# An encoder layer on eight cores: value products behind every attention visit, a plan made with other durations, and one more weight slot

## The chip, the cores and the metric

The program runs on all eight cores of one Trainium2 chip. Every core does the same work on its own two of sixteen sequences; the cores exchange nothing. The metric is the device time in microseconds (us) of the slowest core, as the median of the timed runs. An engine is named as in the profile: PE is the matmul engine (TensorE), ACT ScalarE, DVE VectorE, POOL GpSimd, SP the engine that issues the transfers.

## What is computed

The reference is one layer of an encoder, cut here to its steps. A sequence has 2048 tokens of width 1024.

```
n1 = rmsnorm(h)                         # h: (2048, 1024) a sequence
q, k, v, u, gates = split(n1 @ w_in)    # 8 query heads, 2 key/value heads of 64; u and gates
q, k = rope(rmsnorm(q)), rope(rmsnorm(k))
a = softmax(q k^T / 8) v @ w_attn_up    # every query sees all 2048 keys
p = (multiscale_pool(u) @ pool_w * pool_scale) @ w_pool_up
h = h + (sigmoid(g_a) * a + sigmoid(g_p) * p) @ w_out
h = h + cross_attention(rmsnorm(h), rmsnorm(mem))     # 256 memory tokens, 4 heads of 256
h = h + square(relu(rmsnorm(h) @ w_ff1)) @ w_ff2      # 4096 wide
out = rmsnorm(h)
```

## The kernel before

**Tiles and stages.** Everything is kept with the model's width on the 128 partitions and tokens along the free dimension. A core works on eight blocks of 512 tokens (two sequences, four each). After a prologue (keys, values and pooled input of the first sequence, the folding of the memory into weights) each block goes through stages that the code names A (gates, up and output projections), B (cross attention) and F (the feed-forward layer, FF1 and then FF2). Weights come as fp32 from `wst` the first time or times, are cast to bf16 into a slot of the pool W, stored to `wsc`, and read back from there later. How many blocks read a weight as fp32 before the bf16 copy serves is in the table `LATE`.

**Attention visits.** Attention of a block is cut into 32 visits of 256 keys for two query heads, eight visits to each of four chunks; there are 256 visits in all. A visit (`visit`, in `attention_steps`) has four score matmuls of 64 rows, two at a time side by side (the rows of the trace with `ps<-S_p,KV_p`, x4), into all four PSUM banks of the pool E. One exponential on ACT (line 1242) reads those four banks and writes a tile P in a slot of M2. The value products (`ps<-M_p,KV_p`) multiply P with the values, four matmuls of 64 columns for each visit, two at a time. `GROUP` says after how many visits they are issued: with 2, the products of two visits stand together behind the scores of each second visit, "glued" to them, so that nothing comes between. The next visit's scores write the same four banks and so wait for the exponential of the one before.

**Sums of a softmax.** They are built on DVE, two additions for each visit (lines 1253 and 1254), or on PE as products with ones (`ps<-M_p,ones_bf`). `TAIL_PE` says for which blocks the last visits of each chunk are summed on PE: for block (0, 0) the last two.

**Modes of the array.** Scores use halves of the rows, value products halves of the columns, other matmuls the whole array. `split_columns` looks at PE's finished order: a whole-array operation that comes after value products is issued as two matmuls of 64 columns side by side (line 764), until the next score matmuls; the others are issued whole (line 768).

**What sets the order.** The whole program is recorded as operations, each with a place in a nominal order (`items`): the blocks' stages follow each other, and attention of the next block is laid over them by tables of places (`SHARE`, `SHARE1`, `QUERY`, `TILES`). `schedule` then plays all five engines forward, with a duration for each kind of operation (`act_t`, `dve_t`, `pool_t`, the costs in `copy_any`, `DMA_LAT` for a transfer) and with a random jitter from `SEED`, and gives each engine a fixed order. An operation with several possible engines (casts, additions) goes to the one that the plan finds free. The pools W, M2, M1 and S1 have a fixed number of slots in SBUF, and the plan gives each value its slot. `keep_warm` looks at the finished plan and puts matmuls of ones (`ps<-ones_bf`) into PE's longer planned gaps. The chip runs the five orders with semaphores between them.

Of the kernel before, what the change touches and what calls it, by code (L numbers as in the profile page):

```python
# [49 lines left out]


def GROUP(s, tb):
    return 2


def AUX(query, attention, tile, blocks):

    aux = [(attention(*blocks[0]), ("o1", 0.0), ("o1", 1.0)),
           (query(*blocks[1]), ("o2", 0.0), ("o2", 0.2))]
    steps, k = attention(*blocks[1]), 0  # L60
    for n, lo, hi in SHARE1:
        part, k = steps[k:k + n], k + n
        aux.append((part, lo, hi))
    for b in range(2, 8):
        aux.append((query(*blocks[b]), (f"A{b - 1}", QUERY[0]), (f"A{b - 1}", QUERY[1])))
        steps, k = attention(*blocks[b]), 0
        for n, lo, hi in SHARE:
            part, k = steps[k:k + n], k + n
            aux.append((part, (lo[0] + str(b - 1), lo[1]), (hi[0] + str(b - 1), hi[1])))
    for t, (a, b) in enumerate(TILES):  # L70
        aux.append((tile(t), a, b))
    return aux
# [8 lines left out]
DMA_BW = 380.0  # L81
DMA_FIX = 250.0
BACKLOG = 5000.0
DMA_LAT = 2000.0
DMA_ISSUE = 420.0
ALT_BIAS = 300.0
LEAD0 = 4
SHARE = ((6, ('A', 0.7), ('B', 0.06)), (6, ('B', 0.06), ('F', 0)), (6, ('F', 0), ('F', 0.53)), (16, ('F', 0.53), ('F', 0.958)))
SHARE1 = ((34, ('o2', 0.49), ('F0', 0.988)),)
QUERY = (0.05, 0.42)  # L90
TILES = ((('F1', 0.0), ('F1', 0.31)), (('A2', 0.2), ('F2', 0.0)), (('F2', 0.2), ('F2', 0.41)), (('A3', 0.26), ('A3', 0.94)))
NORM1 = (1, 4)
# [577 lines left out]
def build_core(info=None):  # L670
# [13 lines left out]
    G = Graph()  # L684
    st = ExitStack()
    with st:
        def sb(name, shape, dt):
            return st.enter_context(nc.sbuf_tensor(name, shape, dt))

        SIZES = dict(W=(10, 2048, BF16), M2=(14, 1024, F32), M1=(28, 512, F32), S1=(44, 512, BF16), KV=(4, 2048, BF16))  # L690
        tens = {k: sb(k + "_p", [128, n, w], dt) for k, (n, w, dt) in SIZES.items()}
        ps = st.enter_context(nc.psum_tensor("ps", [128, 8, 512], F32))
        pools = {k: v[0] for k, v in SIZES.items()}
# [89 lines left out]
        def copy_any(dst, src, n, R, W, psum=True, scale=None, engs=("act", "dve", "pool"), rate=1.0):  # L783
            def fn_of(eng):
                def fn(e):
                    if eng == "act":
                        if scale is None:
                            return e.activation(out=dst(), in_=src(), func=AF.Copy)  # L788
                        return e.activation(out=dst(), in_=src(), func=AF.Copy, scale=scale())
                    if scale is None:  # L790
                        return e.tensor_copy(out=dst(), in_=src())  # L791
                    return e.tensor_scalar(out=dst(), in0=src(), scalar1=scale(), scalar2=None, op0=ALU.mult)
                return fn
            fns = {e: fn_of(e) for e in engs}
# [1134 lines left out]
```

How the kernel before makes its waits and increments, by code:

```python
    def do_waits(eng, ws):  # L624
        for w in ws:
            if w[0] == "d":
                eng.wait_ge(dsem[w[1]], w[2])
            else:
                k = ms[w[1]]
                eng.wait_ge(esem[w[1].eng][k // SEM_CAP], k % SEM_CAP + 1)
# [1 line left out]
    def run(e, eng):  # L632
        for o in order[e]:
            if o.mms is not None:
                for m, ws in zip(o.mms, plan[o]):
                    do_waits(eng, ws)
                    ins = m["fn"](eng, "halves" in m)
            else:
                do_waits(eng, plan[o])
                ins = o.fn(eng)
            if o.dma is not None:
                ins.then_inc(dsem[o.key[0]], 16)
            elif o in ms:
                ins.then_inc(esem[e][ms[o] // SEM_CAP], 1)
# [17 lines left out]
    @block.sync  # L662
    def _(eng):
        run("sp", eng)
        for s, c in dcount.items():
            eng.wait_ge(dsem[s], c * 16)
```

## Time and profile before

| | us |
|---|---|
| median of three runs | 2161.4 (2159.53 to 2165.31) |
| the profiled execution | 2164.5 |
| span of its slowest core (core 1) | 2162.9 |
| spans of the eight cores | 2151.9 to 2162.9 |
| PE busy | 2099.0 (97%) |
| DVE, ACT, POOL busy | 1665.7, 1376.6, 402.8 |

The rows of the trace are of core 1. A view "by window" gives the busy time of each engine in a stretch; the time line gives start, length, engine, line, tiles and count of merged instructions, and in brackets the idle time before them with what ended it. Matmuls are pipelined, so a PE row is drawn longer than the time to the next start: durations on PE are read from start to start.

### The profile page before, as it was taken

Reading aid. Unit: us, or ns where it says so; the run is one execution under the profiler, and the core shown is the slowest. Engines: PE = TensorE matmul, PEld = TensorE weight load, DVE = VectorE, ACT = ScalarE, POOL = GpSimd, SP = SyncE. Lnnn points to the kernel's source line nnn. Section 1 sums busy time; section 2 is a strip of 40 time slices with the busy share of each in tenths; the row PEclk is TensorE's granted clock in tenths of the full one; section 3 lists DMA queues with packets and bytes.
Section 4 is the critical chain, followed back from the end, with each engine's and each line's share of the span. In section 5 each row is a group of like instructions: output and inputs, shape, how many; then the busy total and the mean of one; then the engine's idle time right before and its main releaser. Section 6 shows DMA issues by size and latency. Waiting matters only on the chain.

```text
span 2162.9 us, 49417 instructions; the slowest of 8 cores (2151.9 to 2162.9 us)
## 1 busy us (share of the span) xinstructions
PE 2099.0 (97%) x18391; PEld 1210.8 (56%) x18391; DVE 1665.7 (77%) x2358; ACT 1376.6 (64%) x1710; POOL 402.8 (19%) x305
## 2 busy tenths in 40 slices
PE   9898999999999999999999999999999999999998
PEld 5543544445456654566644764467445754476678
DVE  5976788778887798877888778778877788876663
ACT  6787677657965679546775468546764478545431
POOL 1321344222430131003410121002110021000200
PEclk9999999999999999999999999999999999999999
DMA  8977997999777865458634683457534763367446
GB/s 262 315 256 246 312 300 232 304 320 310 249 262 253 280 228 177 165 195 276 231 108 137 224 269 113 137 192 243 182 126 154 256 214 114 134 219 261 135 160 201
DMA packets 152442, 473.29 MB, mean 219 GB/s; under 512 B 17040, under 2 KB 21264, under 8 KB 152208
## 3 DMA queue, kind: packets, MB, share of 16 engines
q1 hardware_dynamic: 152208, 470.14, 66.3%
q8 instruction: 151, 2.47, 0.4%
q14 instruction: 83, 0.68, 0.1%
HBM read 399.82 MB, written 70.25 MB: 217 GB/s over the span
## 4 chain that ended last, share of the span: by engine, by line
PE 82%; DMA 6%; ACT 4%; DVE 4%; issue 3%; SPq 1%; POOL 1%; DVEq 0%; ACTq 0%; POOLq 0%
PE ps L764 44%; PE ps L768 37%; DMA M_p<-wst 4%; ACT M_p L1242 2%; DMA wsc<-W_p 1%; SPq L776 1%; ACT W_p L788 1%; DMA M_p<-pdd 0%; POOL M_p L864 0%; DMA M_p<-xT 0%; ACT M_p L876 0%; DVE M_p L1253 0%; DVE M_p L1254 0%; DVE M_p L881 0%; DVE S_p L1447 0%
## 5 line engine op out<-in xcount | busy, mean ns | idle before, releaser
L1242 ACT ACTIVATE M_p<-ps 128x2048 bf16<-128x2048 f32 x256 | 480.2, 1876 | 265.5 <-PE ps L768 259.2
L764 PE MATMUL ps<-S_p,W_p 128*64 128x512 bf16 (+1 forms) x6136 | 620.3, 357 | 4.0 <-POOL W_p L791 1.4
L764 PEld LDWEIGHTS ps<-S_p,W_p 128*64 128x64 bf16 x6136 | 369.2, 110 | 232.8 <-issue 11.8
L764 PE MATMUL ps<-M_p,W_p 128*64 128x512 bf16 (+1 forms) x4976 | 455.1, 337 | 8.4 <-ACT W_p L788 3.8
L768 PE MATMUL ps<-S_p,W_p 128*128 128x512 bf16 (+1 forms) x2372 | 445.9, 344 | 4.6 <-DVE W_p L791 2.2
L764 PEld LDWEIGHTS ps<-M_p,W_p 128*64 128x64 bf16 x4976 | 310.9, 110 | 133.2 <-issue 14.3
L1253 DVE TENSOR_TENSOR M_p<-M_p 128x1024 f32<-128x1024 f32 x216 | 271.2, 1256 | 114.0 <-ACT M_p L1242 110.0
L864 POOL TENSOR_TENSOR M_p<-M_p 128x512 f32<-128x512 f32 x115 | 164.6, 1433 | 1036.6 <-ACT M_p L855 1001.8
L768 PEld LDWEIGHTS ps<-S_p,W_p 128*128 128x128 bf16 x2372 | 224.7, 98 | 221.6 <-issue 46.9
L1254 DVE TENSOR_TENSOR M_p<-M_p 128x1024 f32<-128x1024 f32 x216 | 281.6, 1304 | 11.4 <-DVE M_p L1253 0.5
L1500 ACT ACTIVATE M_p<-M_p 128x512 bf16<-128x512 f32 x256 | 157.0, 627 | 160.4 <-DVE M_p L1498 158.4
L1498 DVE SCALAR_TENSOR_TENSOR M_p<-ps,M_p 128x512 f32<-128x512 f32 x256 | 174.0, 688 | 66.9 <-PE ps L764 37.2
L791 POOL CAST W_p<-M_p 128x1024 bf16<-128x1024 f32 x96 | 119.6, 1253 | 330.8 <-DMA M_p<-wst 141.8
L768 PE MATMUL ps<-S_p,KV_p 64*128 64x512 bf16 x1024 | 155.1, 381 | 24.9 <-ACT M_p L1242 21.8
L768 PE MATMUL ps<-M_p,W_p 128*128 128x256 bf16 (+1 forms) x1168 | 178.1, 308 | 0.5 <-DVE M_p L1433 0.3
L855 ACT ACTIVATE M_p<-M_p 128x512 f32<-128x512 f32 x216 | 129.5, 624 | 57.5 <-DVE M_p L1402 25.9
L768 PEld LDWEIGHTS ps<-M_p,W_p 128*128 128x128 bf16 x1168 | 111.0, 98 | 65.7 <-issue 16.7
L768 PE MATMUL ps<-M_p,KV_p 128*64 128x512 bf16 x1024 | 136.1, 386 | 0.0
L1322 ACT ACTIVATE M_p<-ps,nbg 128x512 f32<-128x512 f32 x128 | 86.8, 686 | 57.5 <-PE ps L764 54.7
L788 ACT ACTIVATE W_p<-M_p 128x1024 bf16<-128x1024 f32 x72 | 75.4, 1054 | 72.4 <-DMA M_p<-wst 32.1
L1597 DVE TENSOR_TENSOR M_p<-ps,M_p 128x512 f32<-128x512 f32 x112 | 77.1, 688 | 54.1 <-PE ps L764 40.9
L768 PEld LDWEIGHTS ps<-S_p,KV_p 64*128 64x128 bf16 x1024 | 30.2, 94 | 114.2 <-issue 114.2
(105 smaller groups left out, 1985.3 us busy)
## 6 DMA issues: line engine op xcount, KB each, us to landing
W_p<-wsc SPq DMA_DIRECT2D x490, 512.0 KB, 4.7
M_p<-wst SPq DMA_DIRECT2D x182, 512.0 KB, 10.0
wsc<-W_p SPq DMA_DIRECT2D x77, 512.0 KB, 9.4
M_p<-xT SPq DMA_DIRECT2D x120, 256.0 KB, 9.4
outT<-M_p SPq DMA_DIRECT2D x56, 256.0 KB, 5.9
n1d<-M_p SPq DMA_DIRECT2D x28, 256.0 KB, 5.6
M_p<-n1d SPq DMA_DIRECT2D x28, 256.0 KB, 7.2
pdd<-M_p SPq DMA_DIRECT2D x14, 256.0 KB, 3.1
```

Of the source, the lines that this page charges most:

```text
L764: ins = e.matmul(out()[64 * k:64 * k + 64], lhsT=lhsT()[:, 64 * k:64 * k + 64], rhs=rhs(), start=start, stop=stop, skip_group_check=True, ...
L768: return e.matmul(out(), lhsT=lhsT(), rhs=rhs(), start=start, stop=stop, skip_group_check=True, **kw)
L788: return e.activation(out=dst(), in_=src(), func=AF.Copy)
L791: return e.tensor_copy(out=dst(), in_=src())
L855: A(lambda e: e.activation(out=ap(sq), in_=src(), func=AF.Square), 512, False, R, [sq])
L864: TT(lambda e: e.tensor_tensor(out=ap(out), in0=ap(acc), in1=ap(sq), op=ALU.add), [acc, sq], [out])
L1242: A(lambda e: e.activation(out=b16(P).rearrange("p (a n) -> p a n", n=512), in_=ps[:, 0:4, :], func=AF.Exp, scale=0.125), 2048, True, S, [P])
L1253: D(lambda e: e.tensor_tensor(out=ap(acc), in0=ap(acc), in1=lo(), op=ALU.add), 1024, [P, acc], [acc], port=True)
L1254: D(lambda e: e.tensor_tensor(out=ap(acc), in0=ap(acc), in1=hi(), op=ALU.add), 1024, [P, acc], [acc], port=True)
L1322: A(lambda e, b=b, i=i: e.activation(out=ap(Et)[:, i * 512:(i + 1) * 512], in_=ap(b), func=AF.Exp, bias=nbg[:, i * 8 + j:i * 8 + j + 1], s ...
L1498: D(lambda e: e.scalar_tensor_tensor(out=ap(rl), in0=ap(b), scalar=0.0, in1=ap(r), op0=ALU.max, op1=ALU.mult), 512, [b, r], [rl])
L1500: A(lambda e: e.activation(out=hq(H, 2 * hf, 2), in_=ap(rl), func=AF.Square), 512, False, [rl], keys)
```

## The change

`GROUP` becomes 1: the four value products of each visit are issued right behind the scores of the next one. `TAIL_PE` is widened to block (0, 1), whose last four visits of each chunk are summed on PE instead of DVE. The plan gets other durations: `DMA_LAT` 4000 ns instead of 2000, `pool_t` 440 ns instead of 300 for its fixed part, a cast on POOL 380 instead of 200. W has 11 slots instead of 10, S1 40 instead of 44 (the same bytes). The tables of places, `LATE` and `SEED` have other numbers.

```diff
 def GROUP(s, tb):
-    return 2
+    return 1
...
-        for n, lo, hi in SHARE:
+        for n, lo, hi in {2: SHARE2, 3: SHARE3}.get(b, SHARE):
...
-DMA_LAT = 2000.0
+DMA_LAT = 4000.0
...
-SHARE = ((6, ('A', 0.7), ('B', 0.06)), (6, ('B', 0.06), ('F', 0)), (6, ('F', 0), ('F', 0.53)), (16, ('F', 0.53), ('F', 0.958)))
-SHARE1 = ((34, ('o2', 0.49), ('F0', 0.988)),)
-QUERY = (0.05, 0.42)
...
+SLOTS = (11, 14, 28, 40)
+SHARE = ((3, ('A', 0.7), ('B', 0.12)), (9, ('B', 0.12), ('F', 0.12)), (6, ('F', 0.12), ('F', 0.59)), (10, ('F', 0.59), ('F', 0.864)), (6, ('F', 0.864), ('F', 0.958)))
...
+SHARE1 = ((34, ('o2', 0.67), ('F0', 0.965)),)
+QUERY = (0.09, 0.56)
...
-SEED = 7958
+SEED = 194
...
-TAIL_PE = {(0, 0): 2}
+TAIL0 = 2
+TAIL1 = 4
+TAIL_PE = {(0, 0): TAIL0, (0, 1): TAIL1}
...
-LATE.update({("G", i): i % 2 for i in range(8)})
-LATE.update({("FA", i): i % 3 for i in range(16)})
+LATEG = (1, 0, 0, 0, 0, 1, 1, 1)
+LATE.update({("G", i): LATEG[i] for i in range(8)})
+LATEF = (0, 1, 2, 0, 1, 1, 0, 1, 2, 0, 1, 2, 0, 1, 2, 0)
+LATE.update({("FA", i): LATEF[i] for i in range(16)})
...
-        SIZES = dict(W=(10, 2048, BF16), M2=(14, 1024, F32), M1=(28, 512, F32), S1=(44, 512, BF16), KV=(4, 2048, BF16))
+        SIZES = dict(W=(SLOTS[0], 2048, BF16), M2=(SLOTS[1], 1024, F32), M1=(SLOTS[2], 512, F32), S1=(SLOTS[3], 512, BF16), KV=(4, 2048, BF16))
...
         def pool_t(n):
-            return 300.0 + n * 1.9
+            return 440.0 + n * 1.9
...
-            cost = dict(act=act_t(n, psum, scale is not None), dve=dve_t(n, rate), pool=200.0 + n * 0.85)
+            cost = dict(act=act_t(n, psum, scale is not None), dve=dve_t(n, rate), pool=380.0 + n * 0.85)
```

The rows below are of the programs as built, equal instructions merged. Lines of the changed kernel are seven higher (775 for 768, 771 for 764). In the first place, PE in the middle of a block's feed-forward layer, rows with `S_p,KV_p` are the scores of one visit, `M_p,KV_p` value products. Before:

```order
L768 MATMUL ps<-S_p,KV_p 128x512 x4
L768 MATMUL ps<-S_p,W_p 128x512 x16
L768 MATMUL ps<-S_p,KV_p 128x512 x4
L768 MATMUL ps<-M_p,KV_p 64x512 x8
L764 MATMUL ps<-S_p,ones_bf 64x512 x2
L768 MATMUL ps<-S_p,KV_p 128x512 x4
L768 MATMUL ps<-S_p,W_p 128x512 x72
```

PE at the same stage, as changed:

```order
L775 MATMUL ps<-S_p,KV_p 128x512 x4
L775 MATMUL ps<-M_p,KV_p 64x512 x4
L775 MATMUL ps<-M_p,ones_bf 64x512 x2
L771 MATMUL ps<-S_p,W_p 64x512 x16
L775 MATMUL ps<-S_p,KV_p 128x512 x4
L775 MATMUL ps<-M_p,KV_p 64x512 x4
L771 MATMUL ps<-ones_bf 64x512 x6
L771 MATMUL ps<-S_p,W_p 64x512 x32
```

Two visits that stood with only eight value products and a sum between them are no longer there; every score row is followed by four value products, and the weight matmuls between visits are now in the split form.

The second place is PE at the start of attention in the prologue, the first visits of block (0, 0). Before:

```order
L768 MATMUL ps<-S_p,KV_p 128x512 x4
L768 MATMUL ps<-ones_bf 128x512 x8
L768 MATMUL ps<-S_p,KV_p 128x512 x4
L768 MATMUL ps<-M_p,KV_p 64x512 x8
L764 MATMUL ps<-ones_bf 64x512 x8
L768 MATMUL ps<-S_p,KV_p 128x512 x4
L768 MATMUL ps<-ones_bf 128x512 x9
L768 MATMUL ps<-S_p,KV_p 128x512 x4
L768 MATMUL ps<-M_p,KV_p 64x512 x8
L764 MATMUL ps<-S_p,W_p 64x512 x80
```

PE at the same visits, as changed:

```order
L775 MATMUL ps<-S_p,KV_p 128x512 x4
L775 MATMUL ps<-M_p,KV_p 64x512 x4
L771 MATMUL ps<-ones_bf 64x512 x12
L775 MATMUL ps<-S_p,KV_p 128x512 x4
L775 MATMUL ps<-M_p,KV_p 64x512 x4
L771 MATMUL ps<-ones_bf 64x512 x12
L775 MATMUL ps<-S_p,KV_p 128x512 x4
L775 MATMUL ps<-M_p,KV_p 64x512 x4
L771 MATMUL ps<-ones_bf 64x512 x4
L771 MATMUL ps<-S_p,W_p 64x512 x48
```

The value products now stand in every gap, and one visit fewer has no weight matmuls behind it. Ones are still in the gaps.

The third place is DVE in the feed-forward layer of the first block, where weights are still cast. `L1505` reads an FF1 result out of PSUM (`L1498` before), `L1258` and `L1270` belong to the softmax sums and outputs. As changed:

```order
L799 TENSOR_SCALAR S_p<-M_p,vec_sb 128x512
L798 CAST W_p<-M_p 128x1024 x2
L871 TENSOR_TENSOR S_p<-M_p 128x512
L798 CAST W_p<-M_p 128x1024 x4
L1505 SCALAR_TENSOR_TENSOR M_p<-ps,M_p 128x512 x2
L798 CAST W_p<-M_p 128x1024
L1505 SCALAR_TENSOR_TENSOR M_p<-ps,M_p 128x512
L798 CAST W_p<-M_p 128x1024
L1258 TENSOR_TENSOR M_p<-M_p 128x1024
```

DVE at that stage before:

```order
L1254 TENSOR_TENSOR M_p<-M_p 128x1024
L1498 SCALAR_TENSOR_TENSOR M_p<-ps,M_p 128x512 x3
L1253 TENSOR_TENSOR M_p<-M_p 128x1024
L1254 TENSOR_TENSOR M_p<-M_p 128x1024
```

Weight casts have come to DVE (41 without a scale in the program instead of 10, with 69 instead of 96 on POOL and 66 instead of 72 on ACT; two fewer in all), and additions for the softmax sums have left it (400 instead of 432 of lines 1253 and 1254).

## Rows read from the trace of the kernel before

**Rows 1.** The page: span, busy time and share of each engine
```profile
span 2162.9 us, 49417 instructions; the slowest of 8 cores (2151.9 to 2162.9 us)
PE 2099.0 (97%) x18391; PEld 1210.8 (56%) x18391; DVE 1665.7 (77%) x2358; ACT 1376.6 (64%) x1710; POOL 402.8 (19%) x305
```
**Rows 2.** By window: start:end, length, busy us of each engine, clock, DMA share
```profile
0.00:500.00 500.00, 463.75 (x3255) 228.78 (x3257) 381.64 (x500) 361.09 (x455) 142.07 (x114) 0.99 0.90 284
500.00:1200.00 700.00, 686.73 (x6151) 393.48 (x6149) 569.60 (x814) 470.06 (x601) 150.24 (x110) 1.00 0.66 219
1200.00:2163.00 963.00, 948.48 (x8995) 588.56 (x8989) 714.50 (x1046) 545.42 (x655) 110.45 (x81) 1.00 0.55 185
```
**Rows 3.** The page's chain that ended last, by engine
```profile
PE 82%; DMA 6%; ACT 4%; DVE 4%; issue 3%; SPq 1%; POOL 1%; DVEq 0%; ACTq 0%; POOLq 0%
```
**Rows 4.** Waits of PE: waiting <- waited for, us in total, times, longest
```profile
PE ps L768 <- ACT M_p L1242: 21.8, 21, 2.4
PE ps L768 <- DVE W_p L791: 3.8, 5, 1.5
PE ps L764 <- ACT W_p L788: 3.8, 2, 3.0
PE ps L764 <- DMA M_p<-pdd: 2.0, 1, 2.0
PE ps L764 <- DMA W_p<-wsc: 1.6, 2, 1.1
```
**Rows 5.** Time line of PE in a feed-forward layer: start us, length, instructions
```profile
1363.94 0.61 PE L768 MATMUL ps<-S_p,KV_p 64*128 64x512 bf16 x4
1364.48 1.05 PE L768 MATMUL ps<-M_p,KV_p 128*64 128x512 bf16 x8
...
1366.67 0.61 PE L768 MATMUL ps<-S_p,KV_p 64*128 64x512 bf16 x4 [0.93 <-ACT M_p L1242]
1367.27 15.70 PE L768 MATMUL ps<-S_p,W_p 128*128 128x512 bf16 x72
1382.90 0.61 PE L768 MATMUL ps<-S_p,KV_p 64*128 64x512 bf16 x4
1383.44 1.05 PE L768 MATMUL ps<-M_p,KV_p 128*64 128x512 bf16 x8
1384.33 13.98 PE L764 MATMUL ps<-S_p,W_p 128*64 128x512 bf16 x128
1398.24 0.60 PE L768 MATMUL ps<-S_p,KV_p 64*128 64x512 bf16 x4
```
**Rows 6.** Time line of PE in FF2, matmuls of 256 columns
```profile
1434.29 3.66 PE L764 MATMUL ps<-M_p,W_p 128*64 128x256 bf16 x64
1437.88 0.61 PE L768 MATMUL ps<-S_p,KV_p 64*128 64x512 bf16 x4
1438.42 3.67 PE L768 MATMUL ps<-M_p,W_p 128*128 128x256 bf16 x32
1442.02 0.61 PE L768 MATMUL ps<-S_p,KV_p 64*128 64x512 bf16 x4
```
**Rows 7.** Time line of PE at the first visits
```profile
102.23 0.61 PE L768 MATMUL ps<-S_p,KV_p 64*128 64x512 bf16 x4 [1.47 <-ACT M_p L1242]
102.77 2.12 PE L768 MATMUL ps<-ones_bf 128*128 128x512 bf16 x9
107.24 0.61 PE L768 MATMUL ps<-S_p,KV_p 64*128 64x512 bf16 x4 [2.35 <-ACT M_p L1242]
```
**Rows 8.** By source line, duration ns min/median/max; by group: busy us, mean ns
```profile
L1242 ACT ACTIVATE M_p<-ps x256: 1854/1878/1904, 93.5 to 1956.6; 128x2048 bf16<-128x2048 f32 x128
L791 DVE CAST W_p<-M_p x10: 685/694/1017, 18.1 to 439.5; 128x1024 bf16<-128x1024 f32 x10
L1253 DVE TENSOR_TENSOR M_p<-M_p 128x1024 f32<-128x1024 f32 x216 | 271.2, 1256 | 114.0 <-ACT M_p L1242 110.0
L791 POOL CAST W_p<-M_p 128x1024 bf16<-128x1024 f32 x96 | 119.6, 1253 | 330.8 <-DMA M_p<-wst 141.8
```

More of the change, by code:

```diff
@@ L87 @@
 LEAD0 = 4
-SHARE = ((6, ('A', 0.7), ('B', 0.06)), (6, ('B', 0.06), ('F', 0)), (6, ('F', 0), ('F', 0.53)), (16, ('F', 0.53), ('F', 0.958)))
-SHARE1 = ((34, ('o2', 0.49), ('F0', 0.988)),)
-QUERY = (0.05, 0.42)
-TILES = ((('F1', 0.0), ('F1', 0.31)), (('A2', 0.2), ('F2', 0.0)), (('F2', 0.2), ('F2', 0.41)), (('A3', 0.26), ('A3', 0.94)))
+SLOTS = (11, 14, 28, 40)
+SHARE = ((3, ('A', 0.7), ('B', 0.12)), (9, ('B', 0.12), ('F', 0.12)), (6, ('F', 0.12), ('F', 0.59)), (10, ('F', 0.59), ('F', 0.864)), (6, ('F', 0.864), ('F', 0.958)))
+SHARE2 = ((3, ('A', 0.7), ('B', 0.096)), (9, ('B', 0.096), ('F', 0.12)), (6, ('F', 0.12), ('F', 0.47)), (8, ('F', 0.47), ('F', 0.804)), (8, ('F', 0.804), ('F', 0.958)))
+SHARE3 = ((6, ('A', 0.7), ('B', 0.12)), (8, ('B', 0.12), ('F', 0.24)), (4, ('F', 0.24), ('F', 0.47)), (9, ('F', 0.47), ('F', 0.744)), (7, ('F', 0.744), ('F', 0.958)))
+SHARE1 = ((34, ('o2', 0.67), ('F0', 0.965)),)
+QUERY = (0.09, 0.56)
+TILES = ((('F1', 0.1), ('F1', 0.41)), (('A2', 0.2), ('F2', 0.3)), (('F2', 0.1), ('F2', 0.17)), (('A3', 0.22), ('A3', 0.74)))
 NORM1 = (1, 4)
```

## The prediction

> **What bounds the kernel now.** I began with the page: PE is busy for 97% of the span, no other engine for more than 77% [rows 1], and the chain that ended last runs through PE for 82% [rows 3]. So the time is PE's own work plus the places where it stands still. The windows say where: in the first 500 us PE is idle for 500 − 463.75 = 36.3 us, with the DMA engines 90% busy; in the next 700 us for 13.3; in the last 963 for 14.5, the tail after the last matmul among it [rows 2]. To that idle time belong the matmuls of ones that only fill planned gaps. Counted in the program's order there are 220 of them at 0.216 us, 47.5 us. Then the waits of PE: by far the largest is that of a score matmul for the exponential of the visit before, 21.8 us in 21 waits; weights that are cast or loaded too late cost 3.8, 3.8 and 1.6, a load of pooled input 2.0 [rows 4]. The change must be read as: what does it add to PE's work, and which of the stalls does it end?
>
> **PE's work.** Three things change, all counted in the two orders.
>
> Sums of block (0, 1): 4 chunks × 4 visits × 4 matmuls = 64 more, 32 pairs. A pair takes as long as one whole matmul, 0.216 us (below). 32 × 0.216 = **+6.9 us**. On DVE the same visits lose 32 additions of 1.256 us [rows 8], 40 us; DVE isn't the bound, so that counts only where PE waits for it.
>
> Changes of mode: from rows to columns or to the whole array and back. Before, 520; with the change 512. Although value products now stand behind each visit, the count doesn't double: before, a visit without value products had two changes (whole to rows, rows to whole), one with them also two, since what follows value products is issued in split form. Each costs about 0.1 us: four scores take 0.54 us to the next start instead of 2 × 0.216 [rows 5]. 8 × 0.1 = **−0.8 us**.
>
> The split form: 9,491 pairs in the changed program, 5,980 before, so 3,511 matmuls are issued as two. Its price is in the rows. With 512 columns, 72 whole ones go from 1367.27 to 1382.90, 15.63 us, and 64 pairs from 1384.33 to 1398.24, 13.91 us [rows 5]. Less 0.1 for the change of mode that follows each, this is 0.2157 and 0.2158 us. With 256 columns, 64 split ones take 3.59 us and 32 whole ones 3.60 [rows 6]. So **0**, with at most 1 ns either way, 3.5 us, for the range. It has to be 0 in both forms, as nearly the whole program now runs split.
>
> The Trainium skill speaks against this one (TensorEngine Tiling, section Tile-to-Partition Mapping: column tiling disables the fast loading of weights; and TensorE: Matmul & The Clock Gate, section Packing small matmuls: a weight load overlaps running matmuls only where its row group differs, which for column halves it does not). By its figure of 64/1.2 = 53 ns for a load of 64 columns, an exposed load in each of 3,511 more pairs would add 186 us. The rows disagree: the pairs of [rows 5, 6] show no such time, and half the program already ran that way.
>
> **Waits for the exponential.** The scores of a visit use the four banks that the exponential before them reads. From scores to the next scores takes at least 1366.67 − 1363.94 = 2.73 us [rows 5]: 0.54 of scores, 1.88 of exponential [rows 8], the rest semaphores. I take 2.75. Where PE has less real work than that between two score rows, it must stand still or run ones, whatever the rest of the plan does. So I walked both orders with 0.216 us for a matmul or pair of 512 columns, 0.109 for 256 and 0.1 for a change of mode, leaving out the ones. Before, 23 of the 255 gaps between visits fall short, by 20.1 us together. The row that the profile has for it, 21.8 us in 21 waits [rows 4], is that size. Twelve of these 23, 13.2 us, are before 500 us, some with ones in them, as at 102.23 (1.47 us left) and 107.24 (2.35) [rows 7]; the other eleven, 6.9 us, are later and recur from block to block, as at 1366.67 with 0.93 us [rows 5]. With the change 9 gaps fall short, by 8.7 us, all before 200 us. The gain is in two parts: value products of 0.43 us are now in every gap instead of 0.86 in every other one, and the other tables spread the visits. 20.1 − 8.7 = **−11.4 us**. The bounds are 0 (the time is lost to the next wait) and −15, as a wait like that of 2.35 us [rows 7] is longer than the shortfall of its gap.
>
> **Ones.** 195 of them instead of 220, −5.4 us at most. 3.7 of it lie in the same short gaps and are counted above; **−1.7 us** for the rest. They are not work, they stand where the plan sees nothing to do, so this is a hint that the plan has fewer holes and not more than that.
>
> **Transfers, casts and slots.** With 4000 ns for the latency the plan asks for loads earlier, and with an eleventh slot it can. What there is to win is what PE waits for: 2.0 + 1.6 for loads and 3.8 + 3.8 for casts, 11.2 us [rows 4]. A slot of W held by a value is what a load waits for, and a tenth more of them moves a load about a tenth earlier; most waits are for casts in the first 500 us, where the DMA engines are 90% busy [rows 2] and no slot gives them more. The POOL casts are planned at 1.25 us instead of 1.07 and take 1.253 on average [rows 8], so the plan is right about them now on average and moves 27 away. I take **−3 us**, between −11 and +4. The 31 more casts on DVE are 31 × 0.694 = 21.5 us [rows 8] against the 40 that left; **−1 us** for DVE, between −4 and +10. S1 is smaller but free: followed through the changed order, never fewer than 2 of its 40 slots are empty. The bytes read stay the same but for two loads of fp32 weights.
>
> **The sum.** 6.9 − 0.8 + 0 − 11.4 − 1.7 − 3 − 1 = −11.0 us. The profiled execution would take 2164.5 − 11.0 = 2153.5. It is 3.1 above the median, and the difference is taken off that: 2161.4 − 11.0 = **2150.4 us**, 0.5% faster. The cores of one execution span 2151.9 to 2162.9 [rows 1] with the same program, so each term of a few us is at the size of what one core differs from another. What a measurement can tell from no change is about 0.3%, 6.5 us.
>
> **The rivals.** *The gain is given back in the first 500 us.* There the DMA engines are 90% busy and PE idles for 36 us [rows 2] because weights aren't there; the exponential's waits of that stretch (13.2 of the 20.1 us before, 8.7 after) then only turn into waits for weights. What is left is the rest of the spacing, 6.9 us, against 6.9 − 0.8 of new work: −0.8, **2160.6 us**. For it speaks the DMA share, against it that only 11 us of PE's waits name a load or a cast.
>
> *The traced durations mend the early stage too.* If the orders now fit what really happens, part of the 36.3 us of idle time before 500 us and of the ones there goes. With 40% of it, 14.5 us, on top of the sum, it comes to **2136 us**. Against it speaks again the DMA share.
>
> *DVE becomes what PE waits for, in the first feed-forward layer.* Its order there has runs of up to six casts with an addition between them, ahead of the instructions that read FF1's results out of PSUM: 6 × 0.694 + 1.26 = 5.4 us, while PE fills one of four banks in 8 × 0.216 = 1.73 us, so it can run 6.9 us ahead. It decides from the point where a run is late by more than 1.5 us, as DVE is 381.6/500 = 76% busy there [rows 2] and a cast of the fp32 tiles can't start before its load has landed; behind it all results queue. Four or five such stalls of 4 us, 18 us, would make it −11.0 + 18 = +7, **2168.5 us**, slower.
>
> *The split form costs something after all.* At 5 ns for a pair, 3,511 × 5 = 17.6 us, it is slower by more than noise: 2150.4 + 17.6 = **2168 us**; from 3.1 ns on the gain is gone. The rows leave room for 1 ns. An exposed load in each pair, as the skill's rule above has it, would show at once in [rows 5, 6] and has under 1% of this.
>
> *The plan doesn't do what its tables say*: a recorded order is fixed, so value products are where the order shows them; this has no chance of its own.
>
> **How the numbers follow.** My forecast, 2143 to 2157 us around 2150.4, 0.45. Given back in the early stage, 2156 to 2165: 0.26. The early stage mended too, 2130 to 2143: 0.15. DVE: 0.11. The split form: 0.03. From the forecast's case a little falls within 0.3% (above 2154.9), from the second a little below it. Faster by over 0.3%: 0.57. Within: 0.30. Slower: 0.13. The range of 8 in 10 takes in the first three but for the far end of the mended case, and the DVE case at its lower price: 2136 to 2167.
>
> **What would show it.** In the profile after: PE's waits for line 1249 (the exponential) at 9 to 12 us instead of 21.8, and none of about 1 us in the later blocks; 64 pairs of 512 columns still at 13.8 us and the FF2 pieces at 3.6; idle time of PE before 500 us near 33; waits of PE for casts below 8; the later blocks 1 to 2 us shorter each. It would be wrong if PE's waits for DVE lines (1505 above all) grow by over 5 us between 200 and 500 us, if the idle time before 500 us falls by more than 10, or if the waits for the exponential stay at 20 with the gaps filled, which would mean that ACT's own queue, not the spacing, sets them.

## The result, and the profile of the changed kernel

| | before | changed |
|---|---|---|
| median us | 2160.84 (4 runs, 2159.53 to 2165.31) | 2139.34 (4 runs, 2137.71 to 2140.53) |
| ratio | 1 | 0.989, 95% interval 0.9862 to 0.9919 |
| profiled execution | 2164.5 | 2137.7 |
| spans of the eight cores | 2151.9 to 2162.9 | 2126.3 to 2136.1 |

The change makes the kernel 21.5 us faster, 1.0%. The prediction was 2150.4, 11.0 us faster. The profiled executions lie a little above the one median and below the other, so they differ by 26.8. The ratios here and below leave out executions in which the cores of one die show a lower granted clock.

First the page of the changed kernel, against [rows 1, 3, 8]: span, busy time and share of each engine, the chain by engine, and two groups (busy us, mean ns, idle time before them).

```profile
span 2136.1 us, 56390 instructions; the slowest of 8 cores (2126.3 to 2136.1 us)
PE 2096.2 (98%) x21918; PEld 1262.8 (59%) x21918; DVE 1628.9 (76%) x2330; ACT 1386.7 (65%) x1729; POOL 388.0 (18%) x280
...
PE 87%; DVE 5%; DMA 4%; issue 2%; ACT 1%; SPq 1%; DVEq 0%; POOL 0%; ACTq 0%; POOLq 0%
...
L1260 DVE TENSOR_TENSOR M_p<-M_p 128x1024 f32<-128x1024 f32 x200 | 251.1, 1256 | 124.7 <-ACT M_p L1249 121.8
...
L798 POOL CAST W_p<-M_p 128x1024 bf16<-128x1024 f32 x69 | 86.9, 1266 | 279.0 <-DMA M_p<-wst 134.9
```

PE has 19% more instructions but about the same busy time; its share of the chain rose from 82 to 87%. Then the windows of [rows 2] again (length, busy time of PE, PEld, DVE, ACT and POOL, granted clock, DMA share, GB/s).

```profile
0.00:500.00 500.00, 476.48 (x4080) 250.23 (x4082) 358.15 (x503) 368.90 (x470) 117.47 (x93) 1.00 0.93 291
500.00:1200.00 700.00, 694.69 (x7626) 420.60 (x7624) 567.97 (x807) 473.08 (x604) 143.91 (x105) 1.00 0.70 222
1200.00:2140.00 940.00, 925.00 (x10220) 591.97 (x10216) 702.75 (x1022) 544.77 (x657) 126.62 (x83) 1.00 0.57 183
```

PE's idle time before 500 us fell from 36.3 to 23.5 us, though the DMA engines are busier there (0.93 instead of 0.90). From 500 to 1200 us it fell from 13.3 to 5.3. PE's waits (us in total, times, longest), against [rows 4]:

```profile
PE ps L775 <- ACT M_p L1249: 8.1, 11, 1.7
PE ps L771 <- DVE W_p L798: 4.6, 3, 3.1
PE ps L771 <- DMA W_p<-wsc: 3.2, 1, 3.2
PE ps L775 <- ACT S_p L910: 1.7, 2, 1.3
PE ps L771 <- DVE M_p L1604: 1.5, 2, 1.2
...
PE ps L775 <- DVE M_p L1505: 1.4, 3, 0.9
```

The wait for the exponential went from 21.8 to 8.1 us (8.4 with one that another matmul takes). By stage it went from 15.6 to 8.4 before 500 us and from 6.3 to nothing after it. The waits that name a weight's cast or a load are still 7.8 in these rows. All of them, small ones too, are 14.3 before and 9.1 now; all other waits fell from 18.3 to 13.3. A later block, PE's time line, against [rows 5]:

```profile
1364.41 0.60 PE L775 MATMUL ps<-S_p,KV_p 64*128 64x512 bf16 x4
1364.94 0.62 PE L775 MATMUL ps<-M_p,KV_p 128*64 128x512 bf16 x4
1365.40 5.35 PE L771 MATMUL ps<-S_p,W_p 128*64 128x512 bf16 x48
1370.68 0.60 PE L775 MATMUL ps<-S_p,KV_p 64*128 64x512 bf16 x4
1371.21 0.62 PE L775 MATMUL ps<-M_p,KV_p 128*64 128x512 bf16 x4
1371.67 10.53 PE L771 MATMUL ps<-S_p,W_p 128*64 128x512 bf16 x96
1382.13 0.60 PE L775 MATMUL ps<-S_p,KV_p 64*128 64x512 bf16 x4
```

No gap is left in it: 48 pairs, 10.46 us less 0.1 for the change of mode, are 0.216 us each, and the wait of 0.93 us is gone.

**Where the time went.** I took every PE row of the slowest core from its start to the next start, and put into the last line what exceeds the undisturbed duration of its kind (idle time, and rows that run at half the clock):

| us of the slowest core | before | changed |
|---|---|---|
| work of PE, with changes of mode | 2022.5 | 2028.7 (+6.2) |
| ones | 47.5 | 42.1 (−5.4) |
| standing, before 500 us | 49.5 | 33.3 |
| standing, 500 to 1200 us | 20.7 | 11.2 |
| standing, after 1200 us | 12.8 | 11.3 |
| standing, all | 83.1 | 55.8 (−27.3) |

The rest, start and tail, is the same in both. The sum is −26.5, for spans that differ by 26.8. These are the slowest cores of one execution each, but the standing time of every core before is longer than that of any core now.

A part of the standing time is no wait at all. Before, after the wait of 2.35 us at 107.24 [rows 7], PE worked on at half its clock. The windows of before at that place, in the columns of above:

```profile
100.00:108.00 8.00, 4.19 (x27) 1.41 (x25) 7.83 (x10) 5.61 (x5) 1.56 (x2) 1.00 1.00 306
108.00:112.00 4.00, 4.00 (x24) 1.81 (x22) 1.15 (x1) 2.88 (x3) 0.00 (x0) 0.57 0.99 262
112.00:116.00 4.00, 4.00 (x42) 2.08 (x38) 3.56 (x4) 2.32 (x3) 0.00 (x0) 1.00 0.99 278
```

The four busy microseconds from 108 hold 24 matmuls, the next four 42. The granted clock is 0.57 on average, so the lower of the two levels (1.2 of 2.4 GHz) for most of it. Core 1 had four such stretches of 3.4 us before (from 108.1, 193.5, 476.8 and 739.6), each at or just behind a stop of PE of 2.0 to 3.0 us; at half speed they cost at most 4 × 1.7 = 6.8 us. The changed kernel's slowest core has one. On its time line:

```profile
462.41 0.60 PE L775 MATMUL ps<-M_p,ones_bf 128*64 128x512 bf16 x4
466.19 3.45 PE L771 MATMUL ps<-M_p,W_p 128*64 128x512 bf16 x16 [3.18 <-DMA W_p<-wsc]
469.57 0.60 PE L775 MATMUL ps<-S_p,KV_p 64*128 64x512 bf16 x4
```

Eight pairs take 3.38 us instead of 1.73: the wait of 3.18 for a load costs 4.8. But not every stop is followed by such a stretch. The same core's stop of 3.15 us at 212 isn't. Its end on the time line, and the window behind it with clock 1.00:

```profile
214.73 0.62 PE L771 MATMUL ps<-W_p,S_p 128*64 128x512 bf16 x4 [3.15 <-DVE W_p L798]
214.70:219.00 4.30, 3.92 (x32) 1.72 (x34) 3.06 (x5) 2.18 (x2) 1.75 (x2) 1.00 0.68 220
```

Over the eight cores of both executions, 37 stops of PE last 2 us or more (between 50 and 2120 us); 23 of them have a stretch at the lower clock at or within 3.5 us of their end and 14 have none. The slowest cores are extremes: the median of the eight cores has 3.4 us of such losses before and 1.7 now.

### The profile page after: what moved, and what is told of

Its sections match the earlier page's. It is cut to its first block, busy times and chain, and to the rows that moved or that the text cites. A ratio compares the mean times of both kernels' runs of the same rounds, so it can differ in the third digit from the quotient of the medians.

```text
span 2136.1 us, 56390 instructions; the slowest of 8 cores (2126.3 to 2136.1 us)
## 1 busy us (share of the span) xinstructions
PE 2096.2 (98%) x21918; PEld 1262.8 (59%) x21918; DVE 1628.9 (76%) x2330; ACT 1386.7 (65%) x1729; POOL 388.0 (18%) x280
## 4 chain that ended last, share of the span: by engine, by line
PE 87%; DVE 5%; DMA 4%; issue 2%; ACT 1%; SPq 1%; DVEq 0%; POOL 0%; ACTq 0%; POOLq 0%
PE ps L771 71%; PE ps L775 16%; DMA M_p<-wst 2%; DVE M_p L1261 1%; DMA wsc<-W_p 1%; DVE M_p L1260 1%; DMA W_p<-wsc 1%; DMA M_p<-memT 1%; SPq L783 0%; ACT M_p L1249 0%; DVE M_p L1685 0%; DVE W_p L798 0%; DVE M_p L1258 0%; DVE S_p L888 0%; DVE M_p L888 0%
## 5 line engine op out<-in xcount | busy, mean ns | idle before, releaser
L771 PE MATMUL ps<-S_p,W_p 128*64 128x512 bf16 (+1 forms) x10608 | 1035.7, 350 | 6.8 <-DVE W_p L798 1.5
L771 PEld LDWEIGHTS ps<-S_p,W_p 128*64 128x64 bf16 x10608 | 629.2, 110 | 378.5 <-issue 22.1
L1249 ACT ACTIVATE M_p<-ps 128x2048 bf16<-128x2048 f32 x256 | 479.7, 1874 | 259.7 <-PE ps L775 244.0
L771 PE MATMUL ps<-M_p,W_p 128*64 128x512 bf16 (+1 forms) x7168 | 617.0, 326 | 5.0 <-DMA W_p<-wsc 3.2
L771 PEld LDWEIGHTS ps<-M_p,W_p 128*64 128x64 bf16 x7168 | 425.6, 110 | 174.4 <-issue 14.0
L1260 DVE TENSOR_TENSOR M_p<-M_p 128x1024 f32<-128x1024 f32 x200 | 251.1, 1256 | 124.7 <-ACT M_p L1249 121.8
L1261 DVE TENSOR_TENSOR M_p<-M_p 128x1024 f32<-128x1024 f32 x200 | 264.2, 1321 | 9.6 <-DVE M_p L1260 0.5
L1505 DVE SCALAR_TENSOR_TENSOR M_p<-ps,M_p 128x512 f32<-128x512 f32 x256 | 173.0, 685 | 50.9 <-PE ps L771 45.9
L775 PE MATMUL ps<-M_p,KV_p 128*64 128x512 bf16 x1024 | 159.3, 391 | 0.3 <-ACT M_p L1249 0.3
L798 POOL CAST W_p<-M_p 128x1024 bf16<-128x1024 f32 x69 | 86.9, 1266 | 279.0 <-DMA M_p<-wst 134.9
L1604 DVE TENSOR_TENSOR M_p<-ps,M_p 128x512 f32<-128x512 f32 x112 | 76.9, 687 | 49.6 <-PE ps L771 47.8
L795 ACT ACTIVATE W_p<-M_p 128x1024 bf16<-128x1024 f32 x66 | 69.1, 1053 | 61.2 <-DMA M_p<-wst 26.9
L775 PEld LDWEIGHTS ps<-M_p,KV_p 128*64 128x64 bf16 x1024 | 36.4, 108 | 107.5 <-issue 107.1
L1332 ACT ACTIVATE M_p<-M_p 128x1024 f32<-128x1024 f32 x64 | 67.6, 1057 | 4.4
L1334 ACT ACTIVATE M_p<-M_p 128x1024 f32<-128x1024 f32 x64 | 67.4, 1054 | 3.4 <-ACT M_p L1332 0.4
L1409 DVE TENSOR_TENSOR M_p<-ps,M_p 128x512 f32<-128x512 f32 x64 | 44.0, 688 | 30.5 <-PE ps L771 16.5
```

What stands on the lines that cost most here:

```text
L771: ins = e.matmul(out()[64 * k:64 * k + 64], lhsT=lhsT()[:, 64 * k:64 * k + 64], rhs=rhs(), start=start, stop=stop, skip_group_check=True, ...
L775: return e.matmul(out(), lhsT=lhsT(), rhs=rhs(), start=start, stop=stop, skip_group_check=True, **kw)
L1249: A(lambda e: e.activation(out=b16(P).rearrange("p (a n) -> p a n", n=512), in_=ps[:, 0:4, :], func=AF.Exp, scale=0.125), 2048, True, S, [P])
L1260: D(lambda e: e.tensor_tensor(out=ap(acc), in0=ap(acc), in1=lo(), op=ALU.add), 1024, [P, acc], [acc], port=True)
L1261: D(lambda e: e.tensor_tensor(out=ap(acc), in0=ap(acc), in1=hi(), op=ALU.add), 1024, [P, acc], [acc], port=True)
L1505: D(lambda e: e.scalar_tensor_tensor(out=ap(rl), in0=ap(b), scalar=0.0, in1=ap(r), op0=ALU.max, op1=ALU.mult), 512, [b, r], [rl])
```

## The experiments

Three theories stand against each other. *Spacing*: the gain is the filled gaps between score rows. *Durations and slots*: the plan's new latency, POOL durations and the eleventh slot make things ready in time, more than the waits that name them show. *Luck*: any new order with another seed moves the time by as much.

The kernels ran on three other chips; each ratio is to the kernel before on the same chip (medians there 2157.1, 2168.5 and 2167.0). The changed kernel was not run again on these chips, so "against changed" is (ratio − 0.989) × 2161 us, and carries the uncertainty of both ratios, about ±7 us. "Short gaps" is the sum that the walk of the prediction gives for the order. "All waits" adds up the waits of PE on the slowest core of the profiled execution (in e2 7.6 of the 31.2 us name no releaser; PE rows are missing from that core's trace).

| kernel | ratio, 95% | against changed | short gaps | ones | all waits |
|---|---|---|---|---|---|
| before | 1 | +24 | 20.1 | 47.5 | 54.4 |
| changed | 0.989, 0.9862 to 0.9919 | 0 | 8.7 | 42.1 | 30.8 |
| e1 before, all split | 1.0008, 0.9992 to 1.0024 | | 19.8 | 47.5 | 46.7 |
| e2 changed, whole | 0.9987, 0.9974 to 1.0 | +21 | 8.0 | | 31.2 |
| e3 before, GROUP 1 | 1.0091, 1.0066 to 1.0115 | | 15.9 | 52.9 | 52.9 |
| e4 changed, seed 7958 | 0.9932, 0.9908 to 0.9957 | +9 | 6.8 | 40.2 | 34.5 |
| e5 before, seed 194 | 1.0021, 0.9998 to 1.0043 | | 17.9 | 47.7 | 52.0 |
| e6 before, new durations | 0.9988, 0.9975 to 1.0002 | | 16.0 | 47.3 | 54.4 |
| e7 changed, old durations | 1.0002, 0.9986 to 1.0018 | +24 | 13.8 | 44.5 | 52.1 |
| e8 changed, old tables | 1.0016, 0.9992 to 1.004 | +27 | 15.4 | 45.6 | 52.7 |
| e9 changed, old latency | 0.9977, 0.9963 to 0.9992 | +19 | 9.8 | 41.7 | 49.0 |
| e10 changed, old POOL durations | 0.9916, 0.99 to 0.9931 | +6 | 19.1 | 44.7 | 36.2 |
| e11 changed, ten slots | 0.9989, 0.9977 to 1.0002 | +21 | 12.4 | 45.6 | 44.1 |
| e12 changed, no TAIL1 | 0.9958, 0.9942 to 0.9973 | +15 | 15.5 | 54.9 | 36.8 |

### The split form

e1 changes the kernel before so that, from the first scores on, every whole-array operation is issued as halves, as far as the changed kernel goes with it.

```diff
-        if mode == "c" and whole_array(o):
+        if mode != "f" and whole_array(o):
+            mode = "c"
```

> The kernel before in the same order, but the whole-array matmuls behind score matmuls are issued as two column halves too (some 3,670 more split ones, 512 changes of mode instead of 520). Theory that a pair costs what a whole matmul costs: -0.8 us for the changes of mode, so 2155 to 2165 us, no difference. Rival, that a pair costs 2 to 5 ns more: 7 to 18 us slower. Rival, that split matmuls are where the change gained: 10 us faster or more.

Measured 1.0008, no difference. Its PE time line at the place of [rows 5]:

```profile
1358.08 0.61 PE L769 MATMUL ps<-S_p,KV_p 64*128 64x512 bf16 x4 [0.92 <-ACT M_p L1243]
1358.67 15.73 PE L765 MATMUL ps<-S_p,W_p 128*64 128x512 bf16 x144
1374.34 0.60 PE L769 MATMUL ps<-S_p,KV_p 64*128 64x512 bf16 x4
```

72 pairs take 15.67 us to the next start, the 72 whole matmuls of before 15.63. And the wait of 0.92 us stays, as nothing here fills that gap.

e2 takes the split form out of the changed kernel, and so puts a change of mode behind each visit's value products: 788 instead of 512.

```diff
-        if mode == "c" and whole_array(o):
-            for m in o.mms:
-                m["halves"] = True
-        else:
-            mode = o.mms[-1]["mode"]
+        mode = o.mms[-1]["mode"]
```

> The changed kernel in its own order, but everything that can be whole is issued whole, so that PE goes back from columns to the whole array behind each visit's value products: 788 changes of mode instead of 512. At 0.096 us each that is 26.5 us slower than the changed kernel, 2166 us or 0.2% above the kernel before. Rival, that the split form has a price of its own of 2 ns or more: at most 8 us slower than the changed kernel, 2147. The granted clock should not differ.

Measured 0.9987, some 21 us above the changed kernel. Its PE time line:

```profile
1302.63 0.61 PE L771 MATMUL ps<-S_p,KV_p 64*128 64x512 bf16 x4
1303.17 0.62 PE L771 MATMUL ps<-M_p,KV_p 128*64 128x512 bf16 x4
1303.72 1.90 PE L771 MATMUL ps<-M_p,W_p 128*128 128x512 bf16 x7
```

Value products last 0.55 us to the next start instead of 0.46. On the median core of the profiled executions PE's work grew by 25.8 us, 0.093 for each of the 276 changes, while the standing time fell by 11. This fits changes of mode that lie inside waits, which isn't shown place by place. So the split form is what makes GROUP 1 affordable, and no price of it shows.

### Value products behind each visit, alone

```diff
 def GROUP(s, tb):
-    return 2
+    return 1
```

> The kernel before with nothing changed but the value products behind each visit (GROUP 1); the plan is made anew with the old tables, durations and slots. Walked through its order, gaps between visits that are shorter than 2.75 us sum to 15.9 us instead of 19.8, the changes of mode to 0.8 less; ones go up from 220 to 245. Theory of the spacing: -4.7 us, 2156. Theory that issuing value products behind each visit is most of the gain by itself (shorter lives of P, more even work): -15 us or more, 2146 or below. Theory that the plan's other inputs carry the gain: within 5 us of before.

Measured 1.0091: **slower** by 19.7 us, though the walk has 4 us less of short gaps, and the waits for the exponential did fall (21.8 to 13.7 us). The plan made with the old tables got other holes: 245 ones instead of 220 (+5.4 us) and 8.5 us more standing time than before. Together with 0.8 less for changes of mode this is 13.1, about what the profiled spans differ by (12.5); the rest of the 19.7 isn't in the traces. While the waits for the exponential fell by 8, those for DVE, casts left out, rose from 11.3 to 22.8 us: what the spacing gave, DVE's order took. One of its stops, on all eight cores, is this, on PE:

```profile
330.62 0.38 PE L768 MATMUL ps<-M_p,ones_bf 128*64 128x512 bf16 x2
335.17 0.64 PE L764 MATMUL ps<-S_p,ones_bf 128*64 128x512 bf16 x2 [4.17 <-DVE S_p L864]
335.57 0.67 PE L764 MATMUL ps<-ones_bf 128*64 128x512 bf16 x2
336.17 1.03 PE L768 MATMUL ps<-S_p,KV_p 64*128 64x512 bf16 x4
```

and on DVE at that time:

```profile
331.53 2.05 DVE L1251 TENSOR_TENSOR M_p<-M_p 128x1024 f32<-128x1024 bf16 x1
333.50 1.52 DVE L864 TENSOR_TENSOR S_p<-M_p 128x512 bf16<-128x512 f32 x1
```

An addition of a visit stands on DVE ahead of the sum that PE waits for, and the scores after it run at half clock (0.96 us to the next start, not 0.54). The edit that names the change is therefore not by itself the gain. There is no opposite experiment: with GROUP 2 and the other new numbers the plan doesn't fit into its PSUM slots.

### The seed

In the changed kernel `SEED` goes back to 7958 (e4), in the one before it becomes 194 (e5).

```diff
-SEED = 194
+SEED = 7958
```

> The changed kernel with the jitter's seed of the kernel before, all else as changed. Walked through its order: short gaps sum to 6.8 us instead of 8.7, 186 ones instead of 195. Theory that the gain comes from the spacing and the plan's inputs: within 5 us of the changed kernel, 2134 to 2145. Theory that the seed was picked and carries a good part of the gain: 8 us slower or more, 2147 and above.

```diff
-SEED = 7958
+SEED = 194
```

> The kernel before with the changed kernel's seed of the jitter and nothing else. Walked through its order: short gaps sum to 17.9 us instead of 19.8, 221 ones instead of 220. Its distance from the kernel before is what a seed alone does. Theory that a plan's luck is some 5 us: within 0.3%. Theory that the seed is good by itself: 8 us faster or more.

The first costs about 9 us (the intervals just overlap), the second nothing that can be told (+4.5 us). Another seed changes every engine's order, so this is a first measure of what a new order does by chance: under 10 us, from two samples. Losses of 19 and more are over it; one of 6 isn't, and one of 15 is in doubt.

### Durations, tables, slots and TAIL1, each undone alone

```diff
-DMA_LAT = 2000.0
+DMA_LAT = 4000.0
...
-            return 300.0 + n * 1.9
+            return 440.0 + n * 1.9
...
-            cost = dict(act=act_t(n, psum, scale is not None), dve=dve_t(n, rate), pool=200.0 + n * 0.85)
+            cost = dict(act=act_t(n, psum, scale is not None), dve=dve_t(n, rate), pool=380.0 + n * 0.85)
```

e6 makes these edits in the kernel before, e7 takes them back in the changed one.

> The kernel before planned with the changed durations (4000 ns of transfer latency, 440 and 380 ns for GpSimd's fixed part) and nothing else. Walked through its order: short gaps 16.0 us instead of 19.8, 219 ones. Theory that the durations help by what they mend in the spacing: -4 us. Rival, that traced durations mend waits for casts and loads everywhere, whatever the tables: -10 us or more, most of it before 500 us. Rival, that a table tuned under old durations fits new ones badly: slower by up to 10 us.

> The changed kernel planned with the old durations. Walked through its order: short gaps 13.8 us instead of 8.7, 206 ones instead of 195 (+2.4 us). Theory of spacing and planned holes: 7.5 us slower than the changed kernel. Rival, that the durations are the main part of the gain: 12 us slower or more, with more waits for casts and loads.

Added to before they do nothing (−2.6 us, within noise). Taken from the changed kernel, the whole gain is gone. Its first window and its largest waits of PE:

```profile
0.00:500.00 500.00, 461.04 (x3855) 237.68 (x3857) 335.88 (x465) 357.12 (x451) 124.72 (x106) 0.99 0.90 282
```

```profile
PE ps L775 <- ACT M_p L1249: 13.4, 18, 3.3
PE ps L771 <- DVE W_p L798: 6.7, 7, 2.4
```

Idle time of PE before 500 us is 39.0, as bad as before the change. e8 keeps the durations and takes the tables of places, `LATE` and the seed of before.

```diff
...
-SHARE1 = ((34, ('o2', 0.67), ('F0', 0.965)),)
+SHARE1 = ((34, ('o2', 0.49), ('F0', 0.988)),)
-QUERY = (0.09, 0.56)
+QUERY = (0.05, 0.42)
...
-SEED = 194
+SEED = 7958
```

> The changed kernel (GROUP 1, sums of block (0, 1) on PE, new durations, eleventh slot) with the tables of places, LATE numbers and seed of the kernel before. Walked through its order: short gaps 15.4 us instead of 8.7, 211 ones instead of 195 (+3.5 us). Theory of spacing and planned holes: 10 us slower than the changed kernel. Rival, that value products behind each visit fit only with tables spread for them: near or above the kernel before, 20 us slower than the changed one or more.

Measured 1.0016, again the whole gain (of its +27 the seed alone had 9 in e4). Most of it is lost elsewhere than in e7, in the middle:

```profile
500.00:1200.00 700.00, 680.91 (x7253) 414.93 (x7251) 557.39 (x785) 465.11 (x594) 163.65 (x120) 1.00 0.69 218
```

PE idles there for 19.1 us instead of 5.3. Both together show that neither the tables nor the durations hold the gain alone.

e9 and e10 part the durations: only `DMA_LAT = 2000.0`, and only the two POOL costs (300 and 200).

> The changed kernel planned with 2000 ns of transfer latency as before, GpSimd's durations as changed. Walked through its order: short gaps 9.8 us instead of 8.7, 193 ones instead of 195, so by the order alone PE has the same work. Theory that the latency is what the old durations cost (run e7: the whole gain gone): 12 us slower than the changed kernel or more, with waits for loads and for what hangs on them before 500 us. Rival, that GpSimd's durations are: within 5 us of the changed kernel.

> The changed kernel planned with GpSimd's old durations, the latency as changed. Walked through its order: short gaps 19.1 us instead of 8.7, 207 ones instead of 195 (+2.6 us). Theory of spacing and planned holes: 13 us slower than the changed kernel. Rival, that the latency is what counts: within 5 us.

Taking back the latency loses most of it (+19 us), the POOL costs at most a little (+6, no more than a seed). e9 is the telling one. By its order the short gaps are 9.8 us, as good as the changed kernel's. Measured:

```profile
PE ps L775 <- ACT M_p L1249: 14.6, 12, 4.1
```

With 2.9 us that other matmuls wait for the same, it is 17.5. The longest of them, on PE and then on ACT:

```profile
190.93 1.89 PE L771 MATMUL ps<-S_p,W_p 128*64 128x512 bf16 x16
196.90 1.04 PE L775 MATMUL ps<-S_p,KV_p 64*128 64x512 bf16 x4 [4.08 <-ACT M_p L1249]
197.87 1.06 PE L775 MATMUL ps<-M_p,KV_p 128*64 128x512 bf16 x4
```

```profile
189.13 0.59 ACT L795 ACTIVATE S_p<-ps 128x512 bf16<-128x512 f32 x1
193.93 1.06 ACT L795 ACTIVATE W_p<-M_p 128x1024 bf16<-128x1024 f32 x1 [4.22 <-DMA M_p<-wst]
194.90 1.86 ACT L1249 ACTIVATE M_p<-ps 128x2048 bf16<-128x2048 f32 x1
```

The scores at 190 us were done, and ACT was free. But in its fixed order the cast of a weight comes ahead of the exponential, and ACT waited 4.22 us for that weight's load. PE's row says "waits for the exponential"; the cause is a transfer. Then PE runs at half clock: four scores take 0.97 us to the next start. e9's slowest core has up to 10.2 us of such losses, the changed kernel's 1.7 (median of the eight cores 6.0 and 1.7). The same stretch in e9 and, behind it, in the changed kernel:

```profile
190.00:202.00 12.00, 7.92 (x50) 3.10 (x50) 3.87 (x4) 5.19 (x4) 6.51 (x6) 0.72 0.99 298
```

```profile
190.00:202.00 12.00, 11.83 (x102) 4.61 (x98) 8.39 (x11) 9.63 (x12) 0.00 (x0) 1.00 0.85 266
```

What the latency number does to the order is only in part shown. One would think that a plan which believes in 4000 ns asks for loads earlier. The traces don't show that: between 100 and 500 us, 4.8 fp32 weight loads on average were issued and not yet cast in the changed kernel and 4.9 in e9, and before 1200 us ACT waited for such loads for 26.9 and 24.6 us. Loads are late in both; in e9 more of that lateness reaches PE.

e11 has ten slots of W again (and 44 of S1), e12 only the sums of block (0, 0) on PE.

```diff
-SLOTS = (11, 14, 28, 40)
+SLOTS = (10, 14, 28, 44)
```

> The changed kernel with 10 slots of W and 44 of S1 as before. Walked through its order: short gaps 12.4 us instead of 8.7, 211 ones instead of 195 (+3.5 us). Theory of spacing and planned holes: 7 us slower than the changed kernel. Prediction's price of the slot, with loads a tenth later: 1 to 3 us. Rival, that the slot is what ends the early stage's waits: 12 us or more, before 500 us.

```diff
-TAIL_PE = {(0, 0): TAIL0, (0, 1): TAIL1}
+TAIL_PE = {(0, 0): TAIL0}
```

> The changed kernel with the softmax sums of block (0, 1) on DVE as before: 64 matmuls less (-6.9 us of PE's work), 32 additions of 1.26 us more on DVE. Walked through its order: short gaps 15.5 us instead of 8.7 and 254 ones instead of 195 (+12.7 us), so the plan itself sees holes where DVE is late. Theory that the matmuls buy room on DVE: -6.9 + 6.8 + up to 12.7, 7 to 12 us slower than the changed kernel. Prediction's pricing (DVE worth 1 us): 6 us faster.

Ten slots: +21 us. Part of it is lost where no weight is late at all. On all eight cores PE stops and halves its clock between 749 and 763 us; on PE, ACT and DVE of the slowest:

```profile
762.13 2.64 PE L771 MATMUL ps<-M_p,W_p 128*64 128x512 bf16 x16 [4.30 <-ACT M_p L1329]
```

```profile
761.30 1.27 ACT L1329 ACTIVATE M_p<-ps,nbg 128x512 f32<-128x512 f32 x2 [5.38 <-DVE S_p L1382]
```

```profile
754.87 5.72 DVE L1685 SCALAR_TENSOR_TENSOR M_p<-M_p,vec_sb 128x512 f32<-128x512 f32 x7
760.53 0.67 DVE L1382 TENSOR_TENSOR S_p<-M_p 128x512 bf16<-128x512 f32 x1
```

Seven scalings of a finished block's output stand in DVE's order ahead of one sum that the gates and PE need. No slot of W is in this chain; it looks like an accident of this plan, though the run can't exclude that ten slots led to it. So the +21 us are the cost of this kernel with ten slots; how much of it is the slot's own the run doesn't part from such accidents.

Without TAIL1 PE has 6.9 us less work and the kernel is 15 us slower. PE's ones grew by 12.7 us (254 instead of 195) and the standing time by 9.5; the sum of the three is 15.3. DVE, from 200 to 500 us, in e12 and then in the changed kernel (third busy time):

```profile
200.00:500.00 300.00, 288.01 (x2533) 149.22 (x2529) 239.04 (x307) 208.62 (x242) 75.70 (x58) 0.99 0.90 279
```

```profile
200.00:500.00 300.00, 288.97 (x2557) 149.19 (x2555) 210.99 (x290) 206.93 (x242) 64.05 (x49) 0.99 0.93 292
```

DVE is 80% busy instead of 70% there. That the busier DVE is what makes the plan's holes fits this, but the loss lies between what a new order does by chance and what is clearly more.

## Why the prediction was right, and where it fell short

**PE's work, right.** +6.9 for the sums and −0.8 for changes of mode gave +6.1; the trace has +6.2. The split form costs 0 within noise, as the pairs of [rows 5, 6] said and e1 showed: 0.04 us more on 72 pairs, ratio 1.0008. The Trainium skill says that a weight load overlaps running matmuls only where its row group differs (TensorE: Matmul & The Clock Gate, section Packing small matmuls). The prediction read from this that the loads of column halves lie open; e1 doesn't bear that out.

**Waits for the exponential, right in size, half right in cause.** Forecast −11.4, measured −13.4 (21.8 to 8.4). "9 to 12 us, and none of about 1 us in the later blocks" is close to what the rows show. After 500 us, where the DMA share is 0.70 and below, it is nearly exact: −6.9 forecast, −6.3 measured, none left. Yet the later blocks are not 1 to 2 us shorter each, as forecast: after 1200 us the standing time fell by 1.5 in all, with 1.5 and 1.0 us of new waits for DVE lines 1604 and 1270. Before 500 us −4.5 was forecast and −7.2 measured. And the prediction called it spacing, "whatever the rest of the plan does". The order sets only what is lost at least when all else is on time. e9 has nearly the same spacing (9.8) and 17.5 us of this wait; e10 has a walk of 19.1 and 11.2 of wait; ones and other delays may cover the gaps. The walk followed the time in neither.

**Ones.** Forecast −1.7 beside the other terms, −5.4 at most; all 5.4 show in the accounting. The 3.7 that I took as counted already seem not to have been, as the wait fell by more (13.4) than the short gaps did (11.4).

**Transfers, casts and slots, sized too small.** I took −3 and bounded it by −11, "what PE waits for": the rows that name a load or a cast. Those waits fell by 5.2 (14.3 to 9.1, all of them counted; the prediction's 11.2 had only the largest). But these rows aren't all that the step is worth: the time rises by some 19 us when the latency alone is taken from the changed kernel (e9), by 24 with all durations (e7). A late load can show under another name, as a wait for the exponential (e9 at 196.90), since ACT, DVE and POOL each have one fixed order. The bound should have been PE's whole idle time of that stage, and the share of it whose releaser itself had waited for a transfer: `L1249`'s own queue had to be read, not PE's row alone.

**A term that was missing.** The half clock behind some of the stops: at most 6.8 us before, 1.7 after on the slowest cores, −5.1; on the median core 3.4 and 1.7, −1.7. It was there to read in the windows of before, at 108 us.

**DVE.** I took −1 and had slower by DVE at 0.11. The feared wait didn't come: line 1505 costs PE 1.4 us, and all waits for DVE, casts left out, went from 11.3 to 9.7. Relieving it may be worth more: without TAIL1 the time is 15 us higher (e12).

**The rivals.** *Given back in the early stage* is refuted: idle time before 500 us fell by 12.8 us, past the 10 that I had named as the sign of being wrong. *The early stage mended too* (2136 us) was nearest, with 35% of that idle time gone where it supposed 40. Against it I had put the DMA share; it rose to 0.93 while PE's idle time fell. So a high DMA share doesn't say that PE must wait. Which part of the new order mended the stage, the runs don't show; loads aren't asked for earlier in it (4.8 between issue and cast, 4.9 in e9). The time, 2139.3, is inside the range of 2136 to 2167, but outside the 2143 to 2157 of the forecast itself; it lies in the band that had a chance of 0.15. The direction and the mechanism of the spacing were right, the size was half of what came, and that the range still took it in is owed to its width.

**Term by term,** on the slowest cores: work of PE +6.1 forecast, +6.2 measured; waits for the exponential −11.4 and −13.4; ones −1.7 and −5.4; casts and loads −3 and −5.2; all other waits −1 and −5.0; half clock nothing and about −5. No single term holds the missing half: the sum went wrong in small steps, all the same way. (The measured ones add up to −28, not −26.5, presumably because a part of the half clock falls into waits.)

**How it adds up.** Single undoings cost 6 to 27 us each, which is far more together than the 21.5 that there is. Single additions to before give 0 (durations), nothing measurable (seed) and a loss of 19.7 (GROUP 1). So the gain belongs to the combination, and the price of each part, added up, can't give it. The sum of all waits of PE parts these kernels roughly: 30.8 to 36.8 us for the changed one and the three nearest to it, 44 to 54 for the rest. e2, with its 26 us of changes of mode, is off that line, and so is e3, 20 us slower than before with 1.5 us less of waits. What stays open: how much of each single loss is that part's own effect, and how much is the chance of a new order, which two seeds bound only roughly. A rival is untested: if the changed kernel's numbers and seed are the best of many that were tried together, then whatever is undone makes a new and on average worse order, and all seven undoings that made a new order did come out slower, the seed's too. Several seeds for each variant would part the two.

## What to carry to other kernels

A wait's name is the last instruction of a chain: before you bound what a load or a buffer is worth by the waits that name it, look at what stood ahead of the releaser on its own engine, and at how long that had waited. In a kernel whose orders come from a plan, a single changed number shows only what it does in this plan; the price of an edit in one plan isn't its price in another, and the order alone gives only the least that must be lost. Look behind each longer stop of PE for a stretch at half clock too: it made 4.8 us of a stop of 3.18, while a stop of 3.15 on the same core had none.

## What the hardware showed that I had not expected

After a stop of 2.35 us (before, 107 us) the clock was at the lower level for 3.4 us, at one of 3.18 us (changed, 466 us) for as long. At one of 4.08 us (e9, 196 us) it was low from 195.1 to 201.9, 6.8 us, of which PE still stood for 1.8. After 3.15 us (changed, 212 us) it didn't fall at all: of 37 stops of 2 us or more 14 went without. Where the cause lies in the order, the stretch comes on all eight cores at nearly the same place (e3 between 327 and 334 us, e11 between 749 and 763). Elsewhere it differs from core to core of one execution, with losses of 1.7 to 6.8 us before and 1.7 to 5.1 in the changed kernel, whose cores lie some 10 us apart. A change of mode of the array costs 0.093 us where PE is busy; in e2 the standing time fell by about 11 us while the changes added 26.
